# MLP down projection of a hybrid streaming encoder step: pairs of token tiles with seven products of combinations for eight

## What is computed

```python
x = x + mixed @ w_out
h2 = rms_norm(x, ln2)
x = x + jnp.square(jax.nn.relu(h2 @ w_up)) @ w_down
```

## Time and profile before

| what | value |
|---|---|
| median of three runs | 1525.43 us |
| the profiled execution | 1524.6 us, its span 1522.6 us |
| PE busy | 1426.3 us (94%), 7683 matmuls |
| VectorE, ScalarE, GpSimd busy | 731.5 (48%), 419.6 (28%), 83.1 (5%) us |
| mean granted TensorE clock | 0.971 |
| HBM | 78.28 MB read, 9.71 MB written |

### The profile page before, as it was taken

How to read it: one execution, slowest core, us unless ns; L and a number is a source line. 1 busy time by engine, 2 the same in 40 slices (tenths; PEclk the granted TensorE clock), 3 DMA queues, 4 the chain that set the end, 5 groups by cost and what they waited for, 6 DMA issues and landing times.

```text
span 1522.6 us, 19612 instructions
## 1 busy us (share of the span) xinstructions
PE 1426.3 (94%) x7683; PEld 1213.6 (80%) x7691; DVE 731.5 (48%) x1186; ACT 419.6 (28%) x749; POOL 83.1 (5%) x120
## 2 busy tenths in 40 slices
PE   4979999999998993998999999999999999999997
PEld 3764856849577882887989998999889998999886
DVE  6364353544534547664444444444444444444444
ACT  5124233242325556232312211122112211221110
POOL 2510101101000000000000000000000000000000
PEclk7889999999999996999999999999999999999998
DMA  6022423333242113011101110111111110111004
GB/s 187 8 66 74 121 79 99 102 86 92 63 119 53 30 58 126 29 42 56 56 29 56 55 41 17 51 55 41 41 28 55 41 41 28 55 55 41 27 15 125
DMA packets 129547, 92.95 MB, mean 61 GB/s; under 512 B 14679, under 2 KB 119127, under 8 KB 129493
## 3 DMA queue, kind: packets, MB, share of 16 engines
q1 hardware_dynamic: 129492, 92.20, 21.2%
HBM read 78.28 MB, written 9.71 MB: 58 GB/s over the span
## 4 chain that ended last, share of the span: by engine, by line
PE 88%; DVE 4%; DMA 4%; ACT 2%; issue 1%; SPq 1%; POOL 0%; DVEq 0%
PE psum L1496 25%; PE psum L1497 25%; PE psum L1498 25%; DMA k_c<-in_cache_k_dram 3%; PE psum L1730 2%; PE psum L1681 2%; PE psum L1712 1%; PE psum L1715 1%; PE psum L1740 1%; PE psum L1831 1%; PE psum L1562 1%; DVE tops L1219 1%; PE psum L1609 1%; PE psum L1852 0%; POOL rs L709 0%
## 5 line engine op out<-in xcount | busy, mean ns | idle before, releaser
L1464 DVE TENSOR_TENSOR mix<-psum,mix 128x512 f32<-128x512 f32 x288 | 196.4, 690 | 163.4 <-PE psum L1498 163.3
L1496 PE MATMUL psum<-h_hi,wu_hi 128*128 128x384 f32 x768 | 259.3, 338 | 4.2 <-DVE mix L1418 4.2
L1498 PE MATMUL psum<-h_hi,wu_lo 128*128 128x384 f32 x768 | 259.0, 337 | 0.0
L1497 PE MATMUL psum<-h_lo,wu_hi 128*128 128x384 f32 x768 | 259.0, 337 | 0.0
L1496 PE MATMUL psum<-wd_hi,u_hi 128*128 128x512 f32 x576 | 225.4, 391 | 3.6 <-issue 3.6
L1497 PE MATMUL psum<-wd_lo,u_hi 128*128 128x512 f32 x576 | 225.3, 391 | 0.0
L1498 PE MATMUL psum<-wd_hi,u_lo 128*128 128x512 f32 x576 | 225.1, 391 | 0.0
L1496 PEld LDWEIGHTS psum<-h_hi,wu_hi 128*128 128x128 f32 x768 | 145.2, 189 | 4.9 <-issue 4.4
L1497 PEld LDWEIGHTS psum<-h_lo,wu_hi 128*128 128x128 f32 x768 | 145.1, 189 | 0.5
L1498 PEld LDWEIGHTS psum<-h_hi,wu_lo 128*128 128x128 f32 x768 | 145.1, 189 | 0.0
L993 ACT CAST wd_hi<-raw 128x1024 fp32r<-128x1024 f32 x32 | 32.1, 1049 | 401.2 <-PE psum L1498 399.9
(11 more groups left out here) (262 smaller groups left out, 2066.0 us busy)
## 6 DMA issues: line engine op xcount, KB each, us to landing
raw<-in_w_up_dram SPq DMA_DIRECT2D x32, 512.0 KB, 4.5
raw<-in_w_down_dram SPq DMA_DIRECT2D x32, 512.0 KB, 3.4
k_c<-in_cache_k_dram SPq DMA_DIRECT2D x32, 256.0 KB, 3.2
raw<-in_w_in_dram SPq DMA_DIRECT2D x32, 192.0 KB, 4.0
out_dram<-mix SPq DMA_DIRECT2D x9, 512.0 KB
x_in<-in_x_prompt_dram SPq DMA_DIRECT2D x8, 512.0 KB, 4.1
v_c<-in_cache_v_dram SPq DMA_DIRECT2D x16, 256.0 KB, 4.3
kts<-in_cache_v_dram SPq DMA_DIRECT2D x16, 256.0 KB, 3.9
```

The costliest lines, as they stand in the source:

```text
L1464: nc.vector.tensor_tensor(at, psum[:, 4 + 2 * (t % 2) + half, :].rearrange("p (k n) -> p k n", n=P), at, ALU.add).then_inc(y_added, 1)
L1496: nc.tensor.matmul(out, hi(k), r_hi(k), start=first and k == 0, stop=False)
L1497: nc.tensor.matmul(out, hi(k), r_lo(k), start=False, stop=False)
L1498: last = nc.tensor.matmul(out, lo(k), r_hi(k), start=False, stop=end and k == n - 1)
```

## The change

Two token tiles and the two output halves form a pair. With A the squared hidden values (two tiles by two contraction steps: A11, A12, A21, A22) and B the down weights (two contraction steps by two halves: B11, B12, B21, B22), the four output quarters of a pair are formed from seven products where there were eight:

- S1 = A21 + A22, S2 = S1 - A11, S3 = A11 - A21, S4 = A12 - S2
- T1 = B12 - B11, T2 = B22 - T1, T3 = T2 - B11, T4 = B21 - T2
- the products A11 B11, S1 T1, A12 B21, S2 T2, S4 B22, S3 T3, A22 T4.

The residual is kept in combined form over the blocks: two of a pair's four quarters have a third subtracted before block 0 (`part`, 8 operations of 512 elements on VectorE) and added again before the last block (`join`, 8 more). Each product goes into one PSUM bank of five and is added to one or two quarters, 10 additions for a pair. Pairs are the tiles (0, 3), (1, 4), (2, 5) and (6, 7). Tile 8 stays plain with four products in three banks and 4 additions, and the last of the 16 blocks is computed plainly as before, in 18 units of 6 matmuls.

GpSimd forms the combinations in place, in the tiles `up` and `raw`, and the low halves of everything that is computed late (units 4 and 5 of a block, which hold the tiles 6, 7 and 8) and of the second half of the up weights. ScalarE does all the rounding. VectorE forms the other low halves, in the order of `block_adds`; the low half of the up weights (`up_lo(b + 2)`) stands there ahead of S2/S4 and of the two combined weights T3 and T4. The up units of the next block are no longer computed before a down part but cut into pieces of 9 or 6 matmuls between the products of the current one, unit 5 whole at the end. The order of the units becomes token group by token group. PE may use a product's bank once the product five before has been added, and the first five products of a block once all additions of the block before are done. The down weights have their own two slots of `raw`.

```diff
-    u_hi = sb(mlp, "u_hi", [P, 2, 2, T_ALL], F32R)
-    u_lo = sb(mlp, "u_lo", [P, 2, 2, T_ALL], F32R)
...
-    wd_hi = sb(mlp, "wd_hi", [P, 2, D], F32R)
-    wd_lo = sb(mlp, "wd_lo", [P, 2, D], F32R)
-    up = sb(mlp, "up", [P, G, GN])
...
+    u1_hi = sb(mlp, "u1_hi", [P, 7, GN], F32R)
+    u1_lo = sb(mlp, "u1_lo", [P, 7, GN], F32R)
+    u2_hi = sb(mlp, "u2_hi", [P, 7, P], F32R)
+    u2_lo = sb(mlp, "u2_lo", [P, 7, P], F32R)
+    u8_hi = sb(mlp, "u8_hi", [P, 2, P], F32R)
+    u8_lo = sb(mlp, "u8_lo", [P, 2, P], F32R)
+    up = sb(mlp, "up", [P, 4, GN])
+    wd_hi = sb(mlp, "wd_hi", [P, 7, SPAN], F32R)
+    wd_lo = sb(mlp, "wd_lo", [P, 7, SPAN], F32R)
...
+    U_A11, U_A12, U_A22, U_S2, U_S4, U_S3, U_S1 = range(7)
+    W_B11, W_T1, W_B21, W_B22, W_T2, W_T3, W_T4 = range(7)
+    PRODUCTS = 31
+    PAIR_AT = (0, 7, 14, 24)
+    TILE8_AT = 21
+    PAIR_TILES = ((0, 3), (1, 4), (2, 5), (6, 7))
+    PAIR_ADDS = (2, 2, 1, 1, 1, 2, 1)
+    ADDS_OF = PAIR_ADDS * 3 + (2, 1, 1) + PAIR_ADDS
+    ADDS = sum(ADDS_OF)
...
+            def combined(ins, s, value):
+                ins.then_inc(s, 1)
+                pool.wait_ge(s, value)
...
+            def combine_early(b):
+                a11, a12, a21, a22 = up[:, 0, :], up[:, 1, :], up[:, 2, :], up[:, 3, :]
+                b11, b21, first, b22 = raw[:, 2, 0:SPAN], raw[:, 3, 0:SPAN], raw[:, 2, SPAN:], raw[:, 3, SPAN:]
+                pool.wait_ge(u_ready, 4 * b + 2)
+                combined(nc.gpsimd.tensor_tensor(a22, a21, a22, ALU.add), u_combined, 8 * b + 1)
+                pool.wait_ge(wd_ready, 7 * b + 4)
+                combined(nc.gpsimd.tensor_tensor(b22, b22, first, ALU.subtract), wd_combined, 4 * b + 2)
+                combined(nc.gpsimd.tensor_tensor(a21, a11, a21, ALU.subtract), u_combined, 8 * b + 2)
+                combined(nc.gpsimd.tensor_tensor(a11, a22, a11, ALU.subtract), u_combined, 8 * b + 3)
+                combined(nc.gpsimd.tensor_tensor(a12, a12, a11, ALU.subtract), u_combined, 8 * b + 4)
+                combined(nc.gpsimd.tensor_tensor(b11, b22, b11, ALU.subtract), wd_combined, 4 * b + 3)
+                combined(nc.gpsimd.tensor_tensor(b21, b21, b22, ALU.subtract), wd_combined, 4 * b + 4)
...
+            def up_lo(b):
+                pool.wait_ge(wu_rounded, 2 * b + 2)
+                combined(nc.gpsimd.tensor_tensor(wu_lo[:, 1, :, :].rearrange("p k n -> p (k n)"), raw[:, 1, :],
+                                                 wu_hi[:, 1, :, :].rearrange("p k n -> p (k n)").bitcast(F32),
+                                                 ALU.subtract), wu1_ready, b + 1)
...
+            def early_rounded(b, after, up_next):
+                if after is not None:
+                    act.wait_ge(down_done, after + PAIR_AT[2] + 7)
+                act.wait_ge(up_squared, 6 * b + 3)
+                nc.scalar.copy(u1_hi[:, U_A11:U_A12 + 1, :], up[:, 0:2, :]).then_inc(u_rounded, 1)
+                def left(n):
+                    if after is not None:
+                        act.wait_ge(down_done, after + PAIR_AT[3] + n)
...
+                    act.wait_ge(raw_in[2 + k], RAW_DOWN + 16 * b + 16)
+                left(1)
+                down_hi(W_B11, raw[:, 2, 0:SPAN])
+                left(2)
+                act.wait_ge(wd_combined, 4 * b + 1)
+                down_hi(W_T1, raw[:, 2, SPAN:])
+                left(3)
+                down_hi(W_B21, raw[:, 3, 0:SPAN])
+                relu_squared(b, 3, 3)
+                act.wait_ge(up_squared, 6 * b + 4)
+                nc.scalar.copy(u1_hi[:, U_A22, :], up[:, 3, :]).then_inc(u_rounded, 1)
+                left(5)
+                down_hi(W_B22, raw[:, 3, SPAN:])
+                act.wait_ge(wd_combined, 4 * b + 2)
+                down_hi(W_T2, raw[:, 3, SPAN:])
+                act.wait_ge(u_combined, 8 * b + 2)
+                nc.scalar.copy(u1_hi[:, U_S3:U_S1 + 1, :], up[:, 2:4, :]).then_inc(u_rounded, 1)
+                if up_next is not None:
+                    up_hi(up_next, 0)
+                act.wait_ge(u_combined, 8 * b + 4)
+                nc.scalar.copy(u1_hi[:, U_S2:U_S4 + 1, :], up[:, 0:2, :]).then_inc(u_rounded, 1)
+                left(6)
+                act.wait_ge(wd_combined, 4 * b + 3)
+                down_hi(W_T3, raw[:, 2, 0:SPAN])
+                left(7)
+                act.wait_ge(wd_combined, 4 * b + 4)
+                down_hi(W_T4, raw[:, 3, 0:SPAN])
...
+                add(b, TILE8_AT, NT - 1, 0)
+                add(b, TILE8_AT, NT - 1, 1, additions=1)
+                early_a1(b + 1)
+                add(b, TILE8_AT + 1, NT - 1, 1, own=adds_of(TILE8_AT) + 2)
+                add(b, TILE8_AT + 2, NT - 1, 0)
+                add_a11(b, 3)
+                down_lo(b + 1, W_B11, raw[:, 2, 0:SPAN], 1)
+                add_s1(b, 3)
+                add_a12(b, 3)
+                down_lo(b + 1, W_T1, raw[:, 2, SPAN:], 2)
+                down_lo(b + 1, W_B21, raw[:, 3, 0:SPAN], 3)
+                add_s2(b, 3)
+                add_s4(b, 3)
+                if combined:
+                    early_a22(b + 1)
+                else:
+                    u_lo(b + 1, 2, u1_lo[:, U_S3:U_S1 + 1, :], u1_hi[:, U_S3:U_S1 + 1, :], up[:, 2:4, :])
+                down_lo(b + 1, W_B22, raw[:, 3, SPAN:], 4)
+                add_s3(b, 3)
+                add_a22(b, 3)
+                if combined:
+                    down_lo(b + 1, W_T2, raw[:, 3, SPAN:], 5)
+                    early_s31(b + 1)
+                    up_lo(b + 2)
+                    early_s24(b + 1)
+                    down_lo(b + 1, W_T3, raw[:, 2, 0:SPAN], 6)
+                    down_lo(b + 1, W_T4, raw[:, 3, 0:SPAN], 7)
...
+            def product(bank, u_hi, u_lo, w, first, end):
+                nc.tensor.matmul(psum[:, bank, :], u_hi, wd_hi[:, w, :], start=first, stop=False)
+                nc.tensor.matmul(psum[:, bank, :], u_hi, wd_lo[:, w, :], start=False, stop=False)
+                return nc.tensor.matmul(psum[:, bank, :], u_lo, wd_hi[:, w, :], start=False, stop=end)
+            def bank_free(b, n):
+                pe.wait_ge(y_added, 1 + ADDS * b + (adds_of(n - 4) if n >= 5 else 0))
+            def combination(b, q, n, u, w):
+                n += PAIR_AT[q]
+                bank_free(b, n)
...
+            def do_s2(b, q):
+                if q == 0:
+                    pe.wait_ge(u_ready, 4 * b + 4)
+                    pe.wait_ge(wd_ready, 7 * b + 5)
+                combination(b, q, 3, U_S2, W_T2)
...
+            def pair_with(b, q, m):
+                do_a11(b, q)
+                do_s1(b, q)
+                up_part(b + 1, m, 0, 3)
+                do_a12(b, q)
+                do_s2(b, q)
+                up_part(b + 1, m, 3, 6)
+                do_s4(b, q)
+                do_s3(b, q)
+                up_part(b + 1, m, 6, KC)
+                do_a22(b, q)
+            def block_down(b):
+                for q in range(3):
+                    pair_with(b, q, q)
+                tile8_first(b)
+                up_part(b + 1, 3, 0, 3)
+                tile8_last(b)
+                do_a11(b, 3)
+                up_part(b + 1, 3, 3, 6)
+                do_s1(b, 3)
+                do_a12(b, 3)
+                up_part(b + 1, 3, 6, KC)
+                do_s2(b, 3)
+                do_s4(b, 3)
+                up_part(b + 1, 4, 0, 3)
+                do_s3(b, 3)
+                up_part(b + 1, 4, 3, 6)
+                do_a22(b, 3)
+                up_part(b + 1, 4, 6, KC)
+                up_part(b + 1, 5, 0, KC)
...
+            def last_down():
+                b = NFB - 1
+                pe.wait_ge(u_ready, 4 * b + 1)
+                pe.wait_ge(wd_ready, 7 * b + 4)
...
-            mlp_down(NFB - 1, (NFB - 1) % 2, V_MLP + 4 * (NFB - 1) + 4)
+            first_unit(0)
+            turn_h2(NT - 1)
+            first_unit(1)
+            pe.wait_ge(x1_ready, 2 * NT)
+            for m in range(2, 6):
+                first_unit(m)
+            with pe.Fori(0, NFB - 1) as b:
+                block_down(b)
+            last_down()
```

More of the change, by code:

```diff
@@ L991, in down_hi @@
[L991 to L1001, removed]
-                for k in range(2):
[L1003 to L1015, removed]
+                nc.scalar.activation(up[:, into, :], psum[:, up_bank(m), 0:GN], ACT.Relu).then_inc(up_read, 1)
+                act.wait_ge(up_read, n + 1)
@@ new lines, in early_a22, with early_s31, early_s24, half_of @@
+            def early_a22(b):
+                u_lo(b, 2, u1_lo[:, U_A22, :], u1_hi[:, U_A22, :], up[:, 3, :])
+            def early_s31(b):
+                u_lo(b, 3, u1_lo[:, U_S3:U_S1 + 1, :], u1_hi[:, U_S3:U_S1 + 1, :], up[:, 2:4, :])
+            def early_s24(b):
+                u_lo(b, 4, u1_lo[:, U_S2:U_S4 + 1, :], u1_hi[:, U_S2:U_S4 + 1, :], up[:, 0:2, :])
+            def half_of(t, half):
+                return mix[:, 4 * half:4 * half + 4, t * P:(t + 1) * P]
+            def add(b, n, t, half, op=ALU.add, additions=0, own=None):
+                if additions == 0:
```

(39 more changed lines are left out.)

385 lines of the change are left out of this document (274 added, 111 removed).

## The result

The changed kernel takes 1482.09 us (median of 4 runs, 1478.35 to 1485.32) where the kernel before takes 1525.45: ratio 0.9714, with a 95% interval of 0.9696 to 0.9733. I had forecast 1510 us and so 15 us off; it is 43 us. The profiled execution took 1478.35 us, with a span of 1476.6. L numbers from here on are lines of the kernel that the line is from.

The account below looks back on a forecast made before the run. TensorE was taken to bound the MLP loop: 1524.6 us less 40.8 (matmuls) and 6.7 (last block) gives 1477.1, plus 33 of waits at the blocks' sixth products makes 1510 us. Range 1475 to 1532.

Parts of the forecast that it names:

- What bounds the kernel: In the MLP's 15 block steps TensorE alone sets the pace; a step goes from 49.4 to 46.7 us.
- the matmuls removed: Down projection: 96 matmuls a block for 108, 180 fewer over 15 blocks, saving 40.8 us on TensorE's path.
- The last block: Before the last down projection: TensorE's wait (3.7 us) and the half clock behind it (3.0) go, together 6.7 us.
- GpSimd's price: GpSimd's combinations: 2.16 ns an element, so 1.01 us at 384, 1.29 at 512, 2.39 at 1024.
- 4.7 us of hold-up: Block's end: GpSimd stands still during six VectorE subtractions of two SBUF operands, lengthening its chain by 4.7 us.
- with turns the chain would end within 0.3 us of the forecast: Aside on the chain at each block's end: were VectorE also held while GpSimd runs, its end would move at most 0.3 us.
- T0 + 6.0: GpSimd's last combination, T4, was forecast to be out 6.0 us after the block's start, T0.
- 2.1 us in each of 14 blocks: At a block's sixth product TensorE waits 2.1 us for VectorE's first adds, queued behind T4's low half; 33 us with block 0.
- Block 0: First block, with a shorter run-up: TensorE waits 3.7 us at its sixth product.
- Rival 1: No hold-up: GpSimd streams beside VectorE, or its slope is at the lower end; 1477 us, chance 0.25.
- Rival 2: GpSimd at its upper price becomes the bound: stalls of 5.1 us a block, 1555 us, clock falls extra; chance 0.16.
- three-matmul groups: Products' new groups of three matmuls on TensorE: waits priced at nothing, with 9 us as the other bound.

Follow-up runs that it names:

- before_last_early: The kernel before, with only the last block's down weights rounded early, into the up weights' slots: 1518.77 us against 1524.04, ratio 0.9965.
- plus2: The changed kernel with two more GpSimd additions of 384 columns in each block's chain, ahead of T4: 1533.31 us, ratio 1.0062 against the kernel before.
- port: A separate kernel without the layer: six VectorE operations of one kind, alone or beside six GpSimd subtractions; with two SBUF operands GpSimd's six took 10.05 us, alone 7.35.

## Why the prediction was wrong

- **What bounds the kernel, and the matmuls removed: right.** By the program's count 180 fewer; the page has 7511 for 7683, 172 fewer, as some records can be missing from a trace. Steps of 46.82 us (forecast 46.7), pitches unchanged. At 2.63 us for each step without a wait, 15 of them gave 39.4 us, for 40.8 forecast.
- **The last block: right.** The wait and the half clock are gone in the changed kernel's timeline; by itself, in before_last_early, this gave 6.7 us in span and 5.3 (3.4 to 7.3) in medians, for 6.7 forecast.
- **GpSimd's price: right.** 1.03, 1.30 and 2.41 us for 384, 512 and 1024 elements, forecast 1.01, 1.29 and 2.39.
- **"4.7 us of hold-up": the step that failed.** I let GpSimd alone stand still, for the whole of six subtractions. The two engines take turns. What each subtraction cost GpSimd, by the operation that it lengthened, against the forecast: B22 0.38 (0.58), T2 0.32 (0.69), S3/S1 0.58 (0.96), the up weights' 0.85 (0.84), S2/S4 0.59 (0.96). T3's isn't in the chain at all (0.69): VectorE comes to it at 1075.10, behind S2/S4, while T4 already runs, and waits for T4's end. Together 2.75 us, not 4.7. My remark that with turns the chain would end within 0.3 us of the forecast was wrong too: here most turns cost less than the other's whole operation, and T3's none.
- **Small terms on the same path**: the six pauses between GpSimd's operations sum to 0.55 us (0.07 to 0.09 each, one 0.16) and not 0.9, A22's low half came 0.25 earlier, and the seven operations undisturbed take 0.1 more. With 2.0 from the hold-ups these make the 2.5 us between T0 + 6.0 and + 3.5.
- **"2.1 us in each of 14 blocks".** A wait is only what a chain runs past the moment at which its result is wanted. 2.5 us less chain turned 2.1 of waiting into 0.37 of slack, and 33 us into 1.5. The mechanism, its place (sixth product) and its releaser (the add behind T4's low half) were right, as the lengthened chains show; the size of a term was off, in a sum that ended near that moment. The hold-ups alone would have left 0.1 or 0.2 us of waiting; that there is none owes to the small terms, which I did not foresee.
- **Block 0: wrong place.** 3.7 us forecast at its sixth product; 0.29 measured there, and 1.03 at the up weights' low half, where I had put no wait: I had followed block 0's shorter run-up to the sixth product alone.
- **The rivals.** Rival 1 gave the time (1477) by another reason: not that GpSimd streams beside VectorE (it is held), but that it is held for less. Rival 2's clock falls are real once there are waits, and begin at shorter ones, 2.1 us, than the stalls of over 3 us to which I tied them. That three-matmul groups cost nothing was right.

Not settled: why the clock fell after 11 of plus2's 14 equal waits and not after the other three.

## What to carry to other kernels

When a sum of estimates ends near a deadline, price the chain in steps of one more and one fewer of its operations before giving a time: here one operation of 1.0 us divides nothing lost from 19 us, and three divide a gain of 2.9% from a loss of 2.2%. In an in-order queue look first at what stands behind the late operand and doesn't need it; moving the adds ahead of T4's low half recovered some 60 us of a lengthened chain. In these runs GpSimd's work beside VectorE cost nothing where VectorE added from PSUM, and took turns with it where VectorE read two SBUF operands or copied from SBUF to SBUF, so put it under the adds.

## What the runs showed of the hardware that I had not expected

- A VectorE operation with two fp32 SBUF operands and a GpSimd one that reads SBUF hold each other up, and either can be the one that waits: in port 682 to 1570 ns on VectorE, 1.23 to 1.68 us on GpSimd. A VectorE copy from SBUF to SBUF takes part (1304 ns on average beside GpSimd; the first of the six, which started just ahead of GpSimd's, took 0.43 us); with an operand in PSUM there is no effect (680 ns).
- TensorE's granted clock fell after waits of 2.14 us (idle 1.98), from 1.00 to 0.58 in the stretch behind one, and stayed after those of 1.05 and one of 1.73. Even behind those the next spacing is 0.11 us longer than its pitch.
